# Hybrid attention on one Trainium2 core: value products of two steps in a row, a third buffer for turned probabilities, gate products dealt anew

## The reference

```
s = q . k_cmp * scale ;  p_cmp = masked_softmax(s)        # compressed branch, 8 heads, 31 blocks
s = q_rot . k_sel     ;  p = masked_softmax(s)            # selected branch
s = q_rot . k_win     ;  p = masked_softmax(s)            # window branch
out = g0 * p_cmp @ v_cmp + g1 * p_sel @ v_sel + g2 * p_win @ v_win
a = softmax(q1.k1) - lam * softmax(q2.k2) ; o = a @ v     # differential attention, 4 heads
mixer = (sigmoid(gm_a) * (y_nsa @ w_bn) + sigmoid(gm_b) * (y_diff @ w_bd)) @ w_o
```

## Time and profile before

| | |
|---|---|
| median of 3 runs | 1617.99 us (1617.69 to 1618.09) |
| the profiled execution, its own time | 1617.69 us |
| its span in the profile | 1615.9 us |
| TensorE matmuls busy | 1591.8 us, 99% of the span |
| VectorE busy | 1027.2 us, 64% |
| ScalarE busy | 640.2 us, 40% |
| granted TensorE clock, mean | 0.998 of full speed |

### The profile page before, as it was taken

How to read it: one execution, slowest core, us unless ns; L and a number is a source line. 1 busy time by engine, 2 the same in 40 slices (tenths; PEclk the granted TensorE clock), 3 DMA queues, 4 the chain that set the end, 5 groups by cost and what they waited for, 6 DMA issues and landing times.

```text
span 1615.9 us, 21448 instructions
## 1 busy us (share of the span) xinstructions
PE 1591.8 (99%) x8418; PEld 1276.3 (79%) x8418; DVE 1027.2 (64%) x1602; ACT 640.2 (40%) x1144; POOL 83.4 (5%) x139
## 2 busy tenths in 40 slices
PE   7999999999999999999999999999999999999997
PEld 3878777778878888888888877777887888888886
DVE  4597787869885666667576767776668433333344
ACT  2542455455263332222265235545645433232221
POOL 2400000000010011010020000000000000000000
PEclk9999999999999999999999999999999999999999
DMA  9954222255346666665346321112332333334322
GB/s 310 310 163 135 59 61 66 66 157 167 94 120 193 206 189 188 186 209 173 91 142 183 91 66 53 40 40 92 91 91 79 105 92 104 95 101 123 96 86 75
DMA packets 277684, 201.48 MB, mean 125 GB/s; under 512 B 6904, under 2 KB 263216, under 8 KB 276816
## 3 DMA queue, kind: packets, MB, share of 16 engines
q1 hardware_dynamic: 264112, 147.95, 31.5%
q0 software_dynamic: 12608, 43.77, 8.9%
q10 hardware_dynamic: 864, 8.39, 1.3%
HBM read 193.79 MB, written 6.29 MB: 124 GB/s over the span
## 4 chain that ended last, share of the span: by engine, by line
PE 90%; DVE 5%; DMA 3%; ACT 1%; issue 1%; SPq 0%; DVEq 0%; ACTq 0%
PE banks L1762 23%; PE banks L1764 23%; PE banks L1763 23%; PE banks L1944 3%; PE banks L1972 2%; PE banks L1913 2%; DMA ada_first<-in_w_ada_dram 2%; PE banks L1919 1%; PE banks L1850 1%; PE banks L1849 1%; PE banks L1848 1%; PE banks L1923 1%; PE banks L1978 1%; DMA ring<-in_w_in_dram 1%; DVE w_lo L1105 1%; PE banks L1831 1%
## 5 line engine op out<-in xcount | busy, mean ns | idle before, releaser
L1762 PE MATMUL banks<-u_hi,w_hi 128*128 128x512 f32 x1112 | 450.0, 405 | 2.1 <-DVE u_lo L1357 2.1
L1105 DVE TENSOR_TENSOR w_lo<-ring,w_hi 128x1024 fp32r<-128x1024 f32 (+3 forms) x239 | 286.7, 1201 | 253.9 <-ACT w_hi L789 252.5
L1764 PE MATMUL banks<-u_hi,w_lo 128*128 128x512 f32 x1112 | 434.1, 390 | 0.0
L1763 PE MATMUL banks<-u_lo,w_hi 128*128 128x512 f32 x1112 | 433.9, 390 | 0.0
L789 ACT ACTIVATE w_hi<-ring 128x1024 fp32r<-128x1024 f32 (+2 forms) x242 | 250.1, 1033 | 148.0 <-PE banks L1764 86.1
L1762 PEld LDWEIGHTS banks<-u_hi,w_hi 128*128 128x128 f32 x1112 | 209.2, 188 | 45.2 <-issue 5.0
L1764 PEld LDWEIGHTS banks<-u_hi,w_lo 128*128 128x128 f32 x1112 | 208.9, 188 | 44.7
L1763 PEld LDWEIGHTS banks<-u_lo,w_hi 128*128 128x128 f32 x1112 | 209.6, 189 | 36.3
L994 ACT ACTIVATE probs<-banks,neg_max 128x128 f32<-128x128 f32 (+3 forms) x192 | 99.0, 524 | 145.5 <-DVE neg_max L1564 145.5
L1763 PE MATMUL banks<-h_lo,w_hi 128*128 128x512 f32 x352 | 137.0, 389 | 0.0
L1764 PE MATMUL banks<-h_hi,w_lo 128*128 128x512 f32 x352 | 136.9, 389 | 0.0
(11 more groups left out here) (281 smaller groups left out, 2281.5 us busy)
## 6 DMA issues: line engine op xcount, KB each, us to landing
ring<-in_w_ffn_in_dram SPq DMA_DIRECT2D x88, 512.0 KB, 3.9
ada_ring<-in_w_ada_dram POOLq DMA_DIRECT2D x80, 512.0 KB, 4.3
ring<-in_w_in_dram SPq DMA_DIRECT2D x72, 512.0 KB, 3.8
ring<-in_w_ffn_out_dram SPq DMA_DIRECT2D x32, 448.0 KB, 3.4
ada_first<-in_w_ada_dram SPq DMA_DIRECT2D x16, 512.0 KB, 7.5
ring<-in_w_out_dram SPq DMA_DIRECT2D x16, 512.0 KB, 3.6
ring<-in_w_ffn_out_dram SPq DMA_DIRECT2D x16, 512.0 KB, 3.6
w<-in_cmp_w_k_dram SPq DMA_DIRECT2D x8, 512.0 KB, 6.8
```

The source lines that it names most:

```text
L1105: V.tensor_tensor(lo, src, hi.bitcast(fp32), ALU.subtract).then_inc(split_lo, 1)
L1762: M(bank, wh[:, block], sh[:, k, :], start=start, stop=False)
L1763: M(bank, wh[:, block], sl[:, k, :], start=False, stop=False)
L1764: return M(bank, wl[:, block], sh[:, k, :], start=False, stop=stop)
```

## The change

- TensorE does the value products in odd rounds only, from round 3: those of step t-3 and then those of step t-2. An even round has none.
- The turned probabilities go into three buffers in turn, the two halves of `probsT` and the tile `raw`, which is free in this stage. The writers wait for the value products of three steps earlier.
- The 16 extra units: before two in rounds 1, 8 and 39 and one in each of 3, 6, 10, 13, 15, 20, 24, 28, 32 and 36; now one in each even round from 0 to 16, and in 20, 24, 26, 28, 32, 36 and 39.
- The saving of the nsa sums goes from three to four rounds behind, three `add_ada`, two `save_diff` and two `square_diff` go to other rounds, and the `w_lo` of the first gate block is no longer put off.

```diff
-MORE_UNITS = {1: 2, 3: 1, 6: 1, 8: 2, 10: 1, 13: 1, 15: 1, 20: 1, 24: 1, 28: 1, 32: 1, 36: 1, STEPS - 1: 2}
+MORE_UNITS = {0: 1, 2: 1, 4: 1, 6: 1, 8: 1, 10: 1, 12: 1, 14: 1, 16: 1, 20: 1, 24: 1, 26: 1, 28: 1, 32: 1, 36: 1, STEPS - 1: 1}
...
-ADA_STEPS = {t: k for k, t in enumerate((6, 9, 13, 19, 23, 31, 34, 37))}
-DIFF_SAVE = {10: 0, 16: 1, 29: 2}
-DIFF_SQUARE = {12: 0, 18: 1, 30: 2}
-SPLIT_LATER = {2: 4}
+ADA_STEPS = {t: k for k, t in enumerate((6, 9, 13, 20, 23, 29, 34, 37))}
+DIFF_SAVE = {10: 0, 17: 1, 30: 2}
+DIFF_SQUARE = {12: 0, 19: 1, 32: 2}
+SPLIT_LATER = {}
+SAVE_BEHIND = 4
...
+        def turned_probs(s):
+
+            return (probsT[:, 0], probsT[:, 1], raw[:, :, :])[s % 3]
...
-                            act.wait_ge(pv_done, s - 1)
-                            nc.scalar.activation(probsT[:, s % 2, 0, 0:W], turned[:, 0, 0:W], ACT.Copy)\
+                            if s >= 3:
+                                act.wait_ge(pv_done, s - 2)
+                            nc.scalar.activation(turned_probs(s)[:, 0, 0:W], turned[:, 0, 0:W], ACT.Copy)\
...
-                            if s >= 2:
-                                dve.wait_ge(pv_done, s - 1)
+                            if s >= 3:
+                                dve.wait_ge(pv_done, s - 2)
...
-                    if t >= 2:
+                    if t % 2 and t >= 3:
+                        values(l, t - 3)
                         values(l, t - 2)
```

More of the change, by code:

```diff
@@ L1013, in _ @@
                             save_gate(l, m)
-                    if t - 3 in LAST_NSA:
-                        i = SEQUENCE[t - 3][0]
-                        act.wait_ge(pv_done, score_step(l, t - 3) + 1)
+                    if t - SAVE_BEHIND in LAST_NSA:
+                        i = SEQUENCE[t - SAVE_BEHIND][0]
+                        act.wait_ge(pv_done, score_step(l, t - SAVE_BEHIND) + 1)
                         nc.scalar.activation(q_rot[:, :, i * P:(i + 1) * P],
@@ L1575, in copy_turned @@
                             dve.wait_ge(turn_done, turn_step(l, t - 1) + 1)
-                            if s >= 2:
-                                dve.wait_ge(pv_done, s - 1)
+                            if s >= 3:
+                                dve.wait_ge(pv_done, s - 2)
                             h, n = (0, 256) if kind == "cmp" else (1, W)
-                            V.tensor_copy(probsT[:, s % 2, h, 0:n], turned[:, h, 0:n]).then_inc(turn_dve, 1)
+                            V.tensor_copy(turned_probs(s)[:, h, 0:n], turned[:, h, 0:n]).then_inc(turn_dve, 1)
                 def save_diff(i):
@@ L1964, in values @@
                         last = M(nsa_ps[:, c * P:(c + 1) * P], v_cmp[:, g, cols],
-                                 probsT[:, s % 2, 0, g * P:(g + 1) * P], start=c == 0, stop=False,
+                                 turned_probs(s)[:, 0, g * P:(g + 1) * P], start=c == 0, stop=False,
                                  skip_group_check=True)
@@ L1972, in values @@
                                 last = M(nsa_ps[64 * h:64 * h + 64, c * P:(c + 1) * P], v_tok[:, b, v],
-                                         probsT[:, s % 2, h, N * e + b * P:N * e + (b + 1) * P], start=False,
+                                         turned_probs(s)[:, h, N * e + b * P:N * e + (b + 1) * P], start=False,
                                          stop=br == 1 and b == i, skip_group_check=True)
@@ L1978, in values @@
                             last = M(diff_ps[:, P * hd:P * (hd + 1)],
-                                     probsT[:, s % 2, 0, N * e + b * P:N * e + (b + 1) * P],
+                                     turned_probs(s)[:, 0, N * e + b * P:N * e + (b + 1) * P],
                                      vd_tok[:, b, P * hd:P * (hd + 1)], start=b == 0, stop=b == i)
```

## The result

The change made the kernel slower: a median of 1626.26 us (1626.14 to 1626.41, 4 runs) against 1618.04 (1617.69 to 1618.59, 4 runs), a ratio of 1.0051 with a 95% interval of 1.0038 to 1.0063. The forecast was 1627.4 us, between 1620.5 and 1633.1.

A forecast was written before the change was run, and what follows sets the result against it. TensorE was taken to bound the kernel, with value products filling the slack beside the exponentials' chain. Terms 11.8 + 2.4 - 3.3 - 1.2 = +9.7 us on 1617.69 gave 1627.4 us, range 1620.5 to 1633.1.

The forecast's parts named there:

- The floors: Least time from score to next score, through maximum and exponentials: 3.98 us in tile 3, 4.6 in tile 1.
- Even rounds lose their value products: Even attention rounds, left with less TensorE work than their floor, wait for the exponentials: 5.9 us a layer, 11.8 in both.
- All ten rounds named: Rounds 1, 8, 10, 12, 18, 22, 28, 30, 34 and 38, forecast to wait 0.3 to 1.1 us each.
- Late mixes: VectorE extras in even rounds delay the mix, so turns wait 0.1 to 0.6 us: 2.4 us, between nothing and 4.8.
- the refund: A turn that waited is quicker by 0.16 us, 0.86 against 1.02 for eight loads, as its loads are ready.
- Waits of before that go: Earlier waits of turns, differential and few other scores vanish: at most 3.3 us, at least nothing; all of it taken.
- Entering and leaving: TensorE's switches to and from 64-column products: nsa pairs save 0.15 us each, 3.0 in all; other pairs lose; net -1.2 us.
- some 0.3 more: Pairs of nsa followed by differential products, two a layer, lose about 0.3 us each, 1.2 in all.
- The chain of the even rounds: Rival: the even rounds' chain is shorter than its floor, so no new waits: 1613.2 us, chance 0.07.
- The whole switch: Rival: each column-group switch is worth its whole idle stretch, 0.51 us per nsa pair: 1620.2 us, chance 0.07.
- the third rival: VectorE falls behind: extras ahead of the mix delay the next maximum too, old waits stay: up to 1633.1 us, chance 0.12.

## Why the prediction was right

**What bounds.** The floors, read from the timelines before, held to 0.03 us: 3.98 or 3.99 us in rounds 28, 30 and 34 of both layers, 4.14 in round 38 (forecast 4.15), 3.32 to 3.34 in rounds 18 and 22 (forecast 3.34), 4.57 in round 8 (4.6).

**Even rounds lose their value products, 11.8 us.** Measured 11.3 to 11.7, by the waits table above. All ten rounds named did wait, by 1.00 and 0.98 in rounds 8 and 38 and 0.72 behind round 1. Rounds 2 and 6, which I had left out, added 0.05 and some 0.15 a layer. That cover is the cause is shown by the run with the units in even rounds, in which the waits went and the time with them.

**Late mixes, 2.4 us.** The turns' 5.2 us in 14 cases, less 0.05 and the refund of 0.16 each, are 2.3; moving the extras took 2.1 us off. The largest single one, 0.70 in round 3 of layer 0, was behind the split part that is no longer put off; I had not named it. In rounds 21 and 35 the turn waits 0.23 and 0.47 in layer 0, where an `add_ada` stands ahead of the mix, and not at all in layer 1, which has none.

**Waits of before that go, 3.3 us.** By the two waits tables this term cannot be told from the first two, but single rounds show it. In rounds 4 and 5 of layer 0 a score and a turn had waited; they took 7.15 us with four units before and 7.34 with five now, 0.19 more where a unit costs 0.69. So 0.50 went, of which 0.15 is the pair's.

**Entering and leaving, -1.2 us.** This is the term that was mis-sized: 11.3 + 2.3 - 3.3 = 10.3, and the stages grew by 8.1, so what is left for it is -2.2 (-2.6 with the 11.7). The pair of nsa steps is right, 0.15 each: rounds 36 and 37, with five units and no new wait on either side, took 9.50 us before and 9.35 now in both layers. What failed is the step on the other pairs: "some 0.3 more" where nsa is followed by differential products, and 0.06 for each pair of 128-column products. Rounds 24 and 25, before and then after, from the score of 24 to that of 26 (five units in either):

```profile
265.01 0.30 PEld L1919 LDWEIGHTS banks<-kdT,qdT 64*128 64x128 f32 x4 [0.17 <-issue]
...
269.35 0.30 PEld L1919 LDWEIGHTS banks<-kdT,qdT 64*128 64x128 f32 x4 [0.17 <-issue]
...
272.85 0.30 PEld L1919 LDWEIGHTS banks<-kdT,qdT 64*128 64x128 f32 x4
```

```profile
267.51 0.30 PEld L1925 LDWEIGHTS banks<-kdT,qdT 64*128 64x128 f32 x4 [0.17 <-issue]
...
271.05 0.30 PEld L1925 LDWEIGHTS banks<-kdT,qdT 64*128 64x128 f32 x4 [0.36 <-ACT probs L999]
...
275.57 0.30 PEld L1925 LDWEIGHTS banks<-kdT,qdT 64*128 64x128 f32 x4
```

7.84 us before and 8.06 after: 0.22, not 0.3. Rounds 26 and 27, a pair of 128-column products, took 7.29 us before with four units (272.85 to 280.14) and 7.95 now with five (275.57 to 283.52), 0.66 more for a unit that costs 0.69, so nothing for the pair. In tile 0, rounds 6 and 7, the nsa step followed by a differential one cost 0.23 to 0.26 with the wait behind round 6 in it, so rather 0.1. That gives -3.0 + 4 times 0.22, -2.1, or -2.4 with 0.1 in tile 0. Each term was off by at most 1.4 us, and the forecast came out 1.1 us too high.

**The rivals.** The chain of the even rounds was not shorter than its floor. The whole switch as the worth of a pair did not come out: it would have given 1620.2 us. The Trainium skill ("TensorEngine Tiling (Array Packing)", section Tiling Modes) states that a change of tiling mode drains the TensorE; it gives no price, and that every switch costs alike was the forecast's reading. The trace does not bear that reading out: the idle stretch ahead of a score is 0.36 us behind a unit, 0.17 behind 64-column products, and none is shown behind 128-column products (the scores at 196.73 and 292.49 in the rows above). A pair saves only the leaving, since the score that follows is itself such a switch; the run with a unit between pays 0.35 a pair for one more switch in and out. VectorE fell behind by more than 0.16 us only where an extra stood in an even round, and the odd rounds caught up, as the forecast's argument against the third rival had it.

## What to carry to other kernels

Before a block of work is moved out of a round, ask what chain on other engines ran beside it, and add up that chain's floor: here the value products were the half microsecond that hid the exponentials, and a saved switch of 0.15 us was paid with a wait of 0.55. If it is to be moved, other independent work must go where it stood, round by round, which turned +8 us into -4.5 with the same pairs; some 2 of these 4.5 are to be had without pairs too. And extras on an engine that works its queue in order belong into the long rounds, and never ahead of something that the critical engine awaits: two such extras in round 38 took back all that the others had given.

## What the runs showed that I had not expected

Entering a group of 64-column products costs TensorE 0.19 us behind fp32 transposes and 0.32 behind a 512-column product, by load starts, while leaving costs 0.15 ahead of a unit and of a score; that is why a unit between the pair cost 0.35 us and not 0.46. Why the entry behind the transposes is cheaper was not tried. And the kernel before had some 2 us to give by its tables (0.9987, 0.9978 to 0.9996), with no change to its order of value products; that run has the third buffer too, which alone changed nothing that shows.
